# Moving the buffers of a float32r kernel inside the on-chip memory partitions: weight slots to multiples of 1 KB, activations 192 and 448 bytes past one

## What is computed

```python
def first_block(...):                       # 1 layer
    h = rmsnorm(x, g_pre)
    (gq, gk, gv, ga, gz, dq, dk, dv, iq, ik, iw, dz, xq, xz, gates) = split_cols(h @ w_in)   # 1024 x 11352
    ...
    merged = s_gla * (y_gla @ w_gla_out) + s_dsa * (y_dsa @ w_dsa_out) + s_mem * (y_mem @ w_x_out)
    return x + rmsnorm(merged @ w_o, g_post)

def swiglu(h, w_in, w_out):                 # in each of the 2 later layers
    gate, up = jnp.split(h @ w_in, 2, axis=-1)      # 1024 x 5632
    return (jax.nn.silu(gate) * up) @ w_out         # 2816 x 1024

def second_block(...):                      # 2 layers
    mix = jnp.concatenate([main, mo], axis=-1) @ w_out[l]
    x = x + rmsnorm_2(mix, g_mix_post[l])
    x = x + rmsnorm_2(swiglu(rmsnorm_2(x, g_ffn_pre[l]), w_ffn_in[l], w_ffn_out[l]), g_ffn_post[l])
```

## The kernel before, in words

| buffer | start before | past a multiple of 1 KB | start now | past a multiple of 1 KB |
|---|---|---|---|---|
| K | 65664 | 128 | 16512 | 128 |
| raw, whi, wlo | 16512, 32896, 49280 | 128 | 22528, 38912, 55296 | 0 |
| H (hhi, hlo) | 78016 | 192 | 71872 | 192 |
| XR (X, cmhi, cmlo) | 110784 | 192 | 104896 | 448 |
| R (yhi, ahi, alo, shi, slo, xn ...) | 127168 | 192 | 121280 | 448 |
| V | 71424 | 768 | 222656 | 448 |
| gpost, small | 71872, 75968 | 192 | 223104, 227200 | 896 |

## Time and profile before

### The profile page before, as it was taken

One profiled execution on the slowest core, in us unless ns is written; L12 is line 12 of the kernel. 1 busy time (PEld: TensorE's weight loads), 2 busy tenths in 40 slices (PEclk: granted clock), 3 DMA queues, 4 the chain that ended last, 5 costly groups with the idle time before them and its releaser, 6 DMA issues.

```text
span 2001.5 us, 32809 instructions
## 1 busy us (share of the span) xinstructions
PE 1968.7 (98%) x13488; PEld 1781.3 (89%) x13488; DVE 1145.0 (57%) x1595; ACT 932.6 (47%) x1647; POOL 145.5 (7%) x149
## 2 busy tenths in 40 slices
PE   8999999999999999999999999999999999999998
PEld 6798888877889778888999899999988799999998
DVE  3375347465343233353353999972377659999523
ACT  4443142355433342355454755652258856565422
POOL 0000000000000000000000233300000003333000
PEclk9999999999999999999999999999999999999999
DMA  6521122211334123332212233332231113223331
GB/s 179 146 85 64 43 84 84 85 64 59 111 112 162 63 106 105 106 116 89 81 48 80 77 125 106 106 126 95 97 116 43 64 64 116 106 106 106 127 106 64
DMA packets 29824, 191.24 MB, mean 96 GB/s; under 512 B 3689, under 2 KB 4841, under 8 KB 8562
## 3 DMA queue, kind: packets, MB, share of 16 engines
q1 hardware_dynamic: 26562, 178.58, 25.4%
q0 software_dynamic: 3120, 10.62, 2.0%
HBM read 185.38 MB, written 3.67 MB: 94 GB/s over the span
## 4 chain that ended last, share of the span: by engine, by line
PE 90%; DVE 5%; ACT 3%; issue 1%; DMA 1%; SPq 0%; DVEq 0%; ACTq 0%
PE PS L561 21%; PE PS L563 20%; PE PS L562 20%; PE PS L1034 6%; PE PS L1036 6%; PE PS L1035 6%; DVE wlo L2721 1%; ACT whi L1546 1%; PE PS L895 1%; PE PS L714 1%; PE PS L731 1%; PE PS L1152 1%; PE PS L917 1%; PE PS L851 1%; PE PS L1344 1%
## 5 line engine op out<-in xcount | busy, mean ns | idle before, releaser
L2323 DVE TENSOR_TENSOR wlo<-raw,whi 128x2048 fp32r<-128x2048 f32 (+2 forms) x117 | 264.9, 2264 | 375.3 <-ACT whi L1546 374.9
L1546 ACT ACTIVATE whi<-raw 128x2048 fp32r<-128x2048 f32 (+2 forms) x250 | 311.7, 1256 | 211.1 <-PE PS L563 190.7
L561 PE MATMUL PS<-hhi,whi 128*128 128x512 f32 (+1 forms) x768 | 313.2, 408 | 3.1 <-DVE hlo L2370 3.0
L563 PE MATMUL PS<-hhi,wlo 128*128 128x512 f32 (+1 forms) x768 | 302.7, 394 | 0.0
L562 PE MATMUL PS<-hlo,whi 128*128 128x512 f32 (+1 forms) x768 | 301.3, 392 | 0.0
L561 PE MATMUL PS<-whi,ahi 128*128 128x256 f32 x704 | 196.1, 279 | 0.0
L562 PE MATMUL PS<-wlo,ahi 128*128 128x256 f32 x704 | 196.1, 279 | 0.0
L563 PE MATMUL PS<-whi,alo 128*128 128x256 f32 x704 | 196.1, 278 | 0.0
L561 PEld LDWEIGHTS PS<-hhi,whi 128*128 128x128 f32 (+1 forms) x768 | 144.4, 188 | 40.7 <-DVE hlo L2370 5.4
L1034 PE MATMUL PS<-shi,whi 128*128 128x256 f32 x640 | 179.5, 280 | 0.9 <-DVE gated_ L2766 0.4
L1036 PE MATMUL PS<-shi,wlo 128*128 128x256 f32 x640 | 178.5, 279 | 0.0
(11 more groups left out here) (458 smaller groups left out, 4605.8 us busy)
## 6 DMA issues: line engine op xcount, KB each, us to landing
raw<-in_stream SPq DMA_DIRECT2D x165, 1024.0 KB, 4.8
gpost<-in_gposts POOLq DMA_DIRECT2D x5, 512.0 KB, 7.6
X<-in_x SPq DMA_DIRECT2D x4, 512.0 KB, 6.1
X<-in_x POOLq DMA_DIRECT2D x1, 2048.0 KB, 10.4
out<-X SPq DMA_DIRECT2D x4, 512.0 KB, 2.6
bias_line<-linet POOLq DMA_DIRECT2D x1, 1536.0 KB, 35.1
tbias<-bias_line POOLq DMA_DIRECT2D x1, 1024.0 KB, 7.5
memx<-in_mem POOLq DMA_DIRECT2D x1, 1024.0 KB, 5.4
```

Source lines behind the costliest of these rows:

```text
L561: nc.tensor.matmul(out, lh, rh, start=(k == 0), stop=False)
L563: return nc.tensor.matmul(out, ll, rh, start=False, stop=(k == n_k - 1))
L1546: return nc.scalar.activation(out_, in_, func, scale=scale)
L2323: V_.tensor_tensor(wlo[:, s % 2, :, cols_], raw[:, s % 2, :, cols_], whi[:, s % 2, :, cols_], ALU.subtract)\
```

## The change

Only the places of buffers change. `K` goes ahead of the weights, with 256 bytes of filler behind it (`to_kb`), so that `raw`, `whi` and `wlo` start at multiples of 1 KB. 192 bytes of filler (`apart`) stand behind `wlo`, ahead of `H`, and 256 more (`apart_x`) ahead of `XR` and `R`. `V`, `gpost` and `small` go to the end. Every start stays a multiple of 64 bytes. The order of instructions is the same on all engines, row for row, with the same operands and shapes; only line numbers of code behind the declarations move by 8.

```diff
+TO_KB = 64
+APART = 48
...
+        K = sb("K", [P, K_ALL])
+        sb("to_kb", [P, TO_KB])
         raw = sb("raw", [P, 2, KT, C])
         whi = sb("whi", [P, 2, KT, C], F32R)
         wlo = sb("wlo", [P, 2, KT, C], F32R)
-        K = sb("K", [P, K_ALL])
-        V = sb("V", [P, V_COLS])
-        gpost = sb("gpost", [P, D])
-        small = sb("small", [P, 512])
+        sb("apart", [P, APART])
...
+        sb("apart_x", [P, 64])
         place, close = region("XR", 16)
...
         close()
+
+        V = sb("V", [P, V_COLS])
+        gpost = sb("gpost", [P, D])
+        small = sb("small", [P, 512])
```

## The result

The changed kernel takes 2010.49 us (median of 18 executions, 2003.93 to 2018.98) against 1998.26 us before (18, 1993.08 to 2008.87). The ratio is 1.0061, 95% interval 1.0048 to 1.0075: 12 us slower, where 34 us of gain were forecast. It lies under the 1% that the prediction could tell from no change, but with 18 executions on either side its sign is clear.

What follows compares the result with a forecast made beforehand. TensorE, busy 98% of the span, was taken as the bound, through its step from matmul to matmul. Gains of 24.7 us narrow and 9.5 wide, 34.2 together, took the median from 1996.9 to 1963 us, range 1925 to 2017.

Steps and rivals of the forecast that it cites:

- VectorE's and ScalarE's share: Their operations reading the moved buffers, 160 us of the chain: 1.6 us either way if placement changed them 1%, taken as 0.
- the part on H, XR and R: Activation distances from weights go from 64 to 192 or 448 bytes; only this could decide between short and long narrow step.
- the two inner gains: Narrow matmuls all at the short step, 24.7 us, plus wide passes all as short as the shortest, 9.5 us.
- the short step: Narrow matmuls 113.3 ns from start to start, seen in the first layer's second feed-forward half; the long step was 117.7.
- the 388 ns pass: The shortest duration among the wide float32r passes, which ranged from 388 to 394 ns before the change.
- Wide, -9.5 us: Wide matmuls: all 2856 passes fall from a mean near 391.3 to 388 ns, gaining 9.5 us.
- The bound of the loss: Wide matmuls: at worst all passes as long as the longest, 2.7 ns more on each of 2856, 7.7 us.
- Narrow, -24.7 us: Narrow matmuls: all 5606 with the long step go to the short one, 4.4 ns less each, gaining 24.7 us.
- The outer end: Both streams undisturbed: narrow steps fall to 109 ns, 60 us, and wide to 215, 40 us; together 100 us.
- rival 2: The disturbance between matmul streams and weight loads goes: 1932 us with wide steps alone at 215 ns, 1897 with all; chance 0.14.
- Rival 3: Slower: streams meet in every pass, placed in the second feed-forward half and blocked product; 2017 us, or 2053; chance 0.18.
- Rival 1: The matmul streams stay as they are, steps set by timing after a stall or repeating every 64 bytes; 1997 us, chance 0.30.

Runs made afterwards that it cites:

- w0_a64: The changed kernel with all activations moved back to 64 bytes past the weights, which stay at 0 past a KB; ratio 1.0003 to the kernel before.
- h_s_true112: The kernel before with H and the blocked product's sums really starting 112 bytes past the weights, XR and the rest of R at 64; ratio 1.0036.

## Why the prediction was wrong

**What held.** TensorE's step is what the change moves (11.4 us of 12.2 in the wide products alone), and the distance between the streams is what the edit does to it. The alignment of weights, the other buffers, VectorE's and ScalarE's share and the DMA were costed at nothing, and w0_a64 and the new order alone give 1.0003 and 1.0019. The two steps of the second halves are a locked pattern and no fixed price of an address, as the part on H, XR and R said. The prediction's reading of the clock was a little off: the slices read 9 for 90% or more, and there are short stretches at 1.2 GHz in them.

**The step that failed** is the one that priced the two places together: "I take the two inner gains, 24.7 + 9.5 = 34.2 us, since the short step and the 388 ns pass are the only better levels that these very instructions show." The price of a distance was taken from levels that one distance shows, as if the edit would choose the best of them.
- *Wide, -9.5 us.* It was +11.4. The wide steps of before have no chance in them: 229 is the value of distance 64 and 233 that of 192. The bound of the loss, 7.7 us from the longest pass of 394, was too near as well, since the new distance gives a mean of 395 that no row of before had.
- *Narrow, -24.7 us.* No gain came. 64 and 192 are both distances with two possible steps, so the mix stays. Which one a second half has is drawn anew in each execution; the smaller products that repeat cost an estimated 3 us.
- *The outer end, 100 us, and rival 2.* They took 215 and 109 ns from plain float32 as a float32r stream undisturbed. Bare float32r loops of 512 columns never came under 226.6, with no other engine at work, at any distance tried, and with 32 stationary columns too. Of the 14 ns over 215 placement could end 2 to 3.
- *Rival 3* had the right sign and the distance as its cause, "the new distances put the meeting into every pass" (that anything meets isn't shown), but the wrong place: the loss lies in the wide products and not in the feed-forward halves. Chance 0.18 for it was too little, and its 2017 too much, because its larger part, 12.1 us from narrow steps, did not come.
- *Rival 1*, no change, had the narrow part right.

The Trainium skill's page "TensorE: Matmul & The Clock Gate", "Part 2", says that a weight load takes no read bandwidth from the running matmul. For bfloat16 and plain float32 the trace agrees: 215.8 ns at every distance, the page's 215.7. For float32r what I drew from it, that placement does nothing, is refuted by 226.7 to 233.4 ns. Whether a load takes read bandwidth from a float32r stream no run here shows: the distance counts, but a load of 32 columns frees nothing worth naming.

## What to carry to other kernels

A level that a loop shows at one placement says nothing of what another placement gives: sweep the distance in a bare loop first. One profile gave the steps at 16 distances, and the wide steps of whole kernels came within 0.8 ns of them where two entries agreed. When one program shows two speeds in identical stretches, profile it twice before calling either a target. Read each execution's granted clock beside its time before explaining a spread. And look at how busy the next engine is before shortening the first: with VectorE at 94%, pauses took back 6.3 of 12 us.

## What the runs showed of the hardware

- A float32r matmul of 512 columns steps 226.7, 228.9, 232.3 to 233.5, or 233.4 ns when the moving rows start 0, 64, 128 or 192 bytes past the stationary ones (hi and lo buffers alike), with a period of 256 bytes; bfloat16 and plain float32 passes step 215.8 at all four distances.
- A narrow float32r loop (128 stationary, 256 moving columns) at distances 64 and 192 locks into 113.3 or 117.8 ns, can hold it for over 100 us, and can come out otherwise in another execution. At 0 it is 120.0 in every entry.
- Four bytes matter: at distance 4 the wide step is 237.8 and the narrow one with moving activations 123.2 to 123.4, the longest seen but for 126.7 at distance 8 in two of six entries.
- What inside the chip sets these steps isn't settled. That distance counts and absolute place doesn't, is shown for multiples of 64, with weights at 0 and at 128 past a KB. That the distances of neighbouring stream and load alone set the step was tested and fell. The way from one moving row to the next remains an untested rival.
- The granted clock of one kernel's executions lies between 0.992 and 0.999, and the time follows it, by some 7 us over that range in h_s_true112.
